# Attention's norms inside the block of delta rule and attention, and the delta queries' norm folded into the out norm

## What is computed

```python
q = l2norm(q) * (Dh ** -0.5)          # l2norm(x) = x * rsqrt(sum(x*x) + 1e-6)
k = l2norm(k)
v_new = u_i - einsum(w_i, S)
o = einsum(q_i * exp(gc_i), S) + einsum(qk_i, v_new)      # qk = q k^T * decay
S = S * gl_i + einsum(kt_i, v_new)
o_a = rms_norm(o_a, out_norm) * silu(z_a)                 # per head; mean over 128 channels, eps 1e-6
```

## Time and profile before

| | |
|---|---|
| median of three runs | 1382.09 us |
| profiled execution | 1383.11 us, span 1381.3 us |
| busy share of the span: TensorE (matmuls / weight loads) | 90% / 74% |
| VectorE / ScalarE / GpSimd | 62% / 35% / 18% |
| norm block | 374.5 to about 402.5 us |
| block of attention and delta rule | about 402.5 to 509.0 us |
| out norm and output projection | from 509.3 us |

### The profile page before, as it was taken

The page is one execution under the profiler, slowest core; times in us unless marked ns, Lnnn a source line. Parts: engine busy times, 40 slices in busy tenths (PEclk is TensorE's granted clock), DMA queues, the critical chain, the costliest instruction groups (busy, mean ns, idle before and its releaser), DMA issues. The chain is left out here.

```text
span 1381.3 us, 20314 instructions
## 1 busy us (share of the span) xinstructions
PE 1238.8 (90%) x8326; PEld 1017.5 (74%) x8326; DVE 856.2 (62%) x1216; ACT 484.0 (35%) x844; POOL 244.3 (18%) x136
## 2 busy tenths in 40 slices
PE   5999999999968989986999999999972579899898
PEld 4677777888647877875888888887651468788787
DVE  5266873761057767226986856595989869555821
ACT  5234236232235674114243221232834422332500
POOL 2222221221003320003221212222320410000000
PEclk9999999999979999998999999999985679999999
DMA  6322121331130022431233252521210000030423
GB/s 203 47 46 57 31 54 46 108 107 32 45 132 1 2 91 78 153 103 36 78 108 104 65 146 55 183 58 58 61 46 0 2 1 1 3 123 1 168 88 111
DMA packets 117556, 97.77 MB, mean 71 GB/s; under 512 B 37016, under 2 KB 102680, under 8 KB 117336
## 3 DMA queue, kind: packets, MB, share of 16 engines
q1 hardware_dynamic: 103832, 77.46, 18.8%
q10 hardware_dynamic: 13632, 19.01, 4.3%
HBM read 70.24 MB, written 24.51 MB: 69 GB/s over the span
## 5 line engine op out<-in xcount | busy, mean ns | idle before, releaser
L178 PE MATMUL banks<-xt_lo,w_hi 128*128 128x512 f32 x816 | 323.8, 397 | 6.0 <-POOL w_lo L529 6.0
L179 PE MATMUL banks<-xt_hi,w_lo 128*128 128x512 f32 x816 | 320.0, 392 | 0.0
L180 PE MATMUL banks<-xt_hi,w_hi 128*128 128x512 f32 x816 | 319.9, 392 | 0.0
L529 POOL TENSOR_TENSOR w_lo<-features,w_hi 128x1024 fp32r<-128x1024 f32 x55 | 147.6, 2685 | 490.3 <-ACT w_hi L539 490.3
L178 PEld LDWEIGHTS banks<-xt_lo,w_hi 128*128 128x128 f32 x816 | 154.7, 190 | 41.5 <-POOL w_lo L529 6.2
L180 PEld LDWEIGHTS banks<-xt_hi,w_hi 128*128 128x128 f32 x816 | 154.5, 189 | 32.6
L179 PEld LDWEIGHTS banks<-xt_hi,w_lo 128*128 128x128 f32 x816 | 154.8, 190 | 31.4
L588 ACT ACTIVATE temporaries<-banks 128x1024 f32<-128x1024 f32 x47 | 56.0, 1192 | 308.1 <-PE banks L180 297.8
L307 PE MATMUL banks<-temporaries,features 128*128 128x128 f32 x256 | 37.9, 312 | 26.2 <-DVE temporaries L284 26.2
L539 ACT ACTIVATE w_hi<-features 128x1024 fp32r<-128x1024 f32 x55 | 57.8, 1054 | 2.0 <-PEq L203 1.0
L178 PE MATMUL banks<-xt_lo,eout_mh 128*128 128x512 f32 x128 | 51.4, 401 | 5.7 <-DVE xt_lo L1727 4.6
(11 more groups left out here) (533 smaller groups left out, 2482.1 us busy)
## 6 DMA issues: line engine op xcount, KB each, us to landing
features<-in_even_w_in SPq DMA_DIRECT2D x26, 512.0 KB, 4.2
features<-in_odd_w_in SPq DMA_DIRECT2D x25, 512.0 KB, 4.9
features<-in_x SPq DMA_DIRECT2D x8, 512.0 KB, 7.7
even_gates<-temporaries ACTq DMA_DIRECT2D x8, 512.0 KB, 2.7
features<-even_gates SPq DMA_DIRECT2D x8, 512.0 KB, 8.7
features<-in_even_w_out SPq DMA_DIRECT2D x8, 512.0 KB, 3.9
temporaries<-in_x SPq DMA_DIRECT2D x8, 512.0 KB, 4.8
h_between_layers<-features SPq DMA_DIRECT2D x8, 512.0 KB, 2.8
```

The source lines that it names most:

```text
L178: nc.tensor.matmul(out, w[0], x[1], start=start, stop=False)
L179: nc.tensor.matmul(out, w[1], x[0], start=False, stop=False)
L180: return nc.tensor.matmul(out, w[0], x[0], start=False, stop=stop)
L529: nc.gpsimd.tensor_tensor(wl[n % 2], wr[n % NW], wh[n % 2].bitcast(F32), ALU.subtract).then_inc(low, 1)
```

## The change

`norm_blocks` goes. Its work on the four attention queries and the key becomes `swa_norms`, a fourth program in the block of attention and delta rule, with due times from -30 to -2; its list of programs is: clearing of semaphores (GpSimd, due -20), `swa_norms`, `swa_attend`, `gdn_state`. The key is scaled first. The banks for the spreads are two pairs, 4 to 7. Every due time of `swa_attend` behind its preparation is raised by 8. The transposes of its values wait for the value's load, all five scalings and `q_kept`. VectorE's copies and SyncE's copies of the key wait for the scaled key, and SyncE issues the bias copies ahead of them. `gdn_state` waits for `gc_by_head` ahead of its first step.

The delta queries are no longer scaled. Their squares (four on ScalarE, due -5) are summed by 16 small matmuls (due -2.5, in bank 6) and kept as `q_squares`, a 128x256 copy by VectorE (due -2). GpSimd's first scaling of the queries waits for the fourth square. In `delta_norm` VectorE adds `q_squares`, times 128 * 128 * 1e-6, to the sums of the output's squares (due 7.5), and the root is taken of this with scale 1/128 and bias 128 * 1e-12.

Cut to its core:

```diff
-def norm_blocks(co, tag, items, params, fetch=(), ahead=(), late=None, expand=None):
+def swa_norms(co, queries, key, gains, loads, later):
...
+    order = [N - 1] + list(range(N - 1))
+    delta_q = co.at(A_F[0], (HG, T))
+    q_sq = [co.at(at, (T,)) for at in (A_T + 2048, A_BIG + 14400)]
+
+    def sync(sp):
+        yield -30
+        sp.dma_start(*loads[0]).then_inc(key_in, 16)
...
+    def scalar(act):
+        yield -30
+        for n, (x, _) in enumerate(items):
+            if n >= 3:
+                act.wait_ge(summed, n - 2)
+            if x is key:
+                act.wait_ge(key_in, 16)
+            nc.scalar.activation(sq[n % 3], x, ACT.Square).then_inc(squared, 1)
+        yield -28
+        act.wait_ge(summed, N)
+        nc.scalar.activation(rows, co.ps[:, 4, 0:Q], ACT.Sqrt, bias=eps, scale=scale).then_inc(rooted, 1)
+        yield -26
+        act.wait_ge(inverted, 1)
+        for q, (_, of) in enumerate(quarters):
+            nc.scalar.activation(high[:, of], rows, ACT.Copy, scale=own_quarter[:, q:q + 1]).then_inc(high_r, 1)
+        yield -5
+        act.wait_ge(low_r, 4)
+        for h in range(HG):
+            if h >= 2:
+                act.wait_ge(q_summed, h - 1)
+            nc.scalar.activation(q_sq[h % 2], delta_q[:, h, :], ACT.Square).then_inc(q_squared, 1)
+
+    def tensor(pe):
+        yield -30
+        for n in range(N):
+            pe.wait_ge(squared, n + 1)
+            for own, of in quarters:
+                last = nc.tensor.matmul(co.ps[own, 4, 0:Q], co.at(A_CST + C_SUM2 + R - 1 - 2 * n, (R,)), sq[n % 3][:, of], start=n == 0, stop=n == N - 1)
+            last.then_inc(summed, 1)
+        for i, n in enumerate(order):
+            yield -5 + 0.2 * i
+            if i == 0:
+                pe.wait_ge(paired, 1)
+                pe.wait_ge(low_r, 4)
+            if i >= 2:
+                pe.wait_ge(normed, i - 1)
+            for h in range(2):
+                out = co.ps[:, 4 + 2 * (i % 2) + h, :]
+                nc.tensor.matmul(out, pairs[:, n, :], low[:, hs[h]], start=True, stop=False)
+                last = nc.tensor.matmul(out, pairs[:, n, :], high[:, hs[h]], start=False, stop=True)
+            last.then_inc(spread, 1)
+        yield -2.5
+        pe.wait_ge(normed, N - 1)
+        for h in range(HG):
+            pe.wait_ge(q_squared, h + 1)
+            for own, of in quarters:
+                last = nc.tensor.matmul(co.ps[own, 6, 0:Q], co.at(A_CST + C_SUM + R - 1 - h, (R,)), q_sq[h % 2][:, of], start=h == 0, stop=h == HG - 1)
+            last.then_inc(q_summed, 1)
+
+    def vector(dve):
+        yield -30
+        by_head_of(co, co.gc_by_head, co.gc_rows).then_inc(expanded, 1)
+        nc.vector.tensor_copy(pairs.rearrange("p i (m c) -> p (i m) c", c=64), bc(co.at(A_CST + C_ROW, (10,)), 64)).then_inc(paired, 1)
+        yield -28
+        dve.wait_ge(rooted, 1)
+        nc.vector.reciprocal(rows, rows).then_inc(inverted, 1)
+        yield -26
+        dve.wait_ge(inverted, 1)
+        for q, (_, of) in enumerate(quarters):
+            dve.wait_ge(high_r, q + 1)
+            nc.vector.scalar_tensor_tensor(low[:, of], rows, own_quarter[:, q:q + 1], high[:, of].bitcast(F32), ALU.mult, ALU.subtract).then_inc(low_r, 1)
+        for i, n in enumerate(order):
+            yield -5 + 0.2 * i
+            x, gain = items[n]
+            dve.wait_ge(spread, i + 1)
+            v = x.rearrange("p (h t) -> p h t", h=2)
+            nc.vector.scalar_tensor_tensor(v, v, gain, co.ps[:, 4 + 2 * (i % 2):6 + 2 * (i % 2), :], ALU.mult, ALU.mult).then_inc(normed, 1)
+        yield -2
+        dve.wait_ge(q_summed, HG)
+        nc.vector.tensor_copy(co.q_squares, co.ps[:, 6, 0:Q]).then_inc(q_kept, 1)
+
+    return dict(sync=sync, scalar=scalar, tensor=tensor, vector=vector, q_squared=(q_squared, HG), q_kept=(q_kept, 1), key_normed=(normed, 1), all_normed=(normed, N), value_in=(value_in, 16), gates_in=(gates_in, 16 * len(loads[2:])),
...
-def gdn_state(co):
+def gdn_state(co, expanded, q_squared):
...
+            if c == 0:
+                pool.wait_ge(*q_squared)
...
+                if c < 0:
+                    pe.wait_ge(*expanded)
...
-def swa_attend(co, sinks, zb, ahead):
+def swa_attend(co, sinks, zb, ahead, norms, late):
...
     def sync(sp):
         yield -9
-            sp.dma_start(kd[64 * h:64 * h + 64, 1 - h, 64:], kb[64 - 64 * h:128 - 64 * h, :]).then_inc(moved, 16)
-        for h in range(2):
+        sp.wait_ge(*norms["key_normed"])
+        for h in range(2):
+            sp.dma_start(kd[64 * h:64 * h + 64, 1 - h, 64:], kb[64 - 64 * h:128 - 64 * h, :]).then_inc(moved, 16)
...
-            yield 10 * n + 2
+            yield late + 10 * n + 2
     def tensor(pe):
-        yield -9
+        yield late - 9
+        pe.wait_ge(*norms["value_in"])
+        pe.wait_ge(*norms["all_normed"])
+        pe.wait_ge(*norms["q_kept"])
-                yield 10 * n + 1
+                yield late + 10 * n + 1
...
-                yield 10 * n + (2 if n >= 0 else 8)
+                yield late + 10 * n + (2 if n >= 0 else 8)
...
-                yield 10 * n + 6
+                yield late + 10 * n + 6
...
     def vector(dve):
-        yield -9
+        yield late - 9
+        dve.wait_ge(*norms["key_normed"])
-        yield -2.5
+        yield late - 2.5
...
-                yield 10 * n + 1
+                yield late + 10 * n + 1
+                if n == 1:
+                    dve.wait_ge(*norms["gates_in"])
-                yield 10 * n + 2
+                yield late + 10 * n + 2
-                yield 10 * n + (3 if n >= 0 else 8)
+                yield late + 10 * n + (3 if n >= 0 else 8)
...
         yield -10
-        yield -7
+        yield late - 7
-                yield 10 * n + (6 if n >= 0 else 8)
+                yield late + 10 * n + (6 if n >= 0 else 8)
-                yield 10 * n + 7
+                yield late + 10 * n + 7
...
-    scale, eps = (co.at(A_CST + C_PARAM + 2 + i, (1,)) for i in range(2))
-    squared, summed, rooted, inverted, high_r, low_r, spread, gated = (
-        co.sem(f"eo_{n}") for n in ("squared", "summed", "rooted", "inverted", "high_r", "low_r", "spread", "gated"))
+    squared, summed, joined, rooted, inverted, high_r, low_r, spread, gated = (
+        co.sem(f"eo_{n}") for n in ("squared", "summed", "joined", "rooted", "inverted", "high_r", "low_r", "spread", "gated"))
     def scalar(act):
...
         yield 8
-        act.wait_ge(summed, N)
-        nc.scalar.activation(rows, co.ps[:, 6, 0:Q], ACT.Sqrt, bias=eps, scale=scale).then_inc(rooted, 1)
+        act.wait_ge(joined, 1)
+        nc.scalar.activation(rows, rows, ACT.Sqrt, bias=co.at(co.eps_at[HEAD * RMS_EPS * L2_EPS], (1,)), scale=1.0 / HEAD).then_inc(rooted, 1)
         yield 11
...
+        yield 7.5
+        dve.wait_ge(summed, N)
+        nc.vector.scalar_tensor_tensor(rows, co.q_squares, HEAD * HEAD * RMS_EPS, co.ps[:, 6, 0:Q], ALU.mult, ALU.add).then_inc(joined, 1)
         yield 9
...
-    co.pairs_r = co.rounded("pairs", A_T + 3072, (5, P))
-    co.eps_at = {RMS_EPS: A_MISC + 568, GN_EPS: A_MISC + 569, 128 * L2_EPS: A_MISC + 570, 64 * RMS_EPS: A_MISC + 571}
+    co.pairs_r = co.rounded("pairs", A_BIG + 13504, (5, P))
+    co.q_squares = co.at(A_T + 3600, (T // 4,))
+    co.eps_at = {RMS_EPS: A_MISC + 568, GN_EPS: A_MISC + 569, 128 * L2_EPS: A_MISC + 570, 64 * RMS_EPS: A_MISC + 571, HEAD * RMS_EPS * L2_EPS: A_MISC + 572}
         def _(pool):
...
-    norm_blocks(co, "eq", [(x_, 64, qn, None) for x_ in qb] + [(kb, 64, kn, None)] + [(x_, 128, 1.0, None) for x_ in q], 0, late=(kb, kvb[0]), expand=(co.gc_by_head, co.gc_rows),
-                fetch=[(vb, kvb[1])] + [(zb[b], zg[WB + b]) for b in range(WB)] + [(za[b], zg[b]) for b in range(WB)])
-    side_by_side(co, swa_attend(co, a["swa_sinks"][0], co.at(A_F[6], (WB, T)), w_ahead), gdn_state(co))
+    cleared = clearing(co, at=-20)
+    norms = swa_norms(co, qb, kb, (qn, kn), [(kb, kvb[0]), (vb, kvb[1])] + [(zb[b], zg[WB + b]) for b in range(WB)], [(za[b], zg[b]) for b in range(WB)])
+    side_by_side(co, cleared, norms, swa_attend(co, a["swa_sinks"][0], co.at(A_F[6], (WB, T)), w_ahead, norms, 8), gdn_state(co, norms["expanded"], norms["q_squared"]))
```

More of the change, by code:

```diff
@@ L654, in _ @@
             aside.upto(NB)
-def norm_blocks(co, tag, items, params, fetch=(), ahead=(), late=None, expand=None):
+def swa_norms(co, queries, key, gains, loads, later):
     nc = co.nc
-    old = co.old_sems() if late is not None else []
     R, Q = 32, T // 4
+    items = [(x, gains[0]) for x in queries] + [(key, gains[1])]
+    N = len(items)
     sq = [co.at(A_T + 1024 * i, (T,)) for i in range(3)]
@@ L668, in norm_blocks @@
     high, low = co.row_parts
-    scale, eps = (co.at(A_CST + C_PARAM + 2 * params + i, (1,)) for i in range(2))
-    first_row = np.cumsum([0] + [P // item[1] for item in items]).tolist()
-    hot, pairs = co.hot_r, co.pairs_r
+    scale, eps = (co.at(A_CST + C_PARAM + i, (1,)) for i in range(2))
+    pairs = co.pairs_r
```

(24 more changed lines are left out.)

8 lines of the change are left out of this document (4 added, 4 removed).

## The result

| | before | after |
|---|---|---|
| median of seven runs | 1382.09 us (1380.71 to 1388.08) | 1390.69 us (1387.81 to 1395.62) |
| ratio after / before, 95% interval | | 1.0057 (1.0038 to 1.0076) |
| profiled execution (span) | 1383.11 (1381.3) | 1393.11 (1391.3) |
| first square of the norms to the end of the last gating | 134.45 | 143.10 |
| the span without that stretch | 1246.9 | 1248.2 |

The change makes the kernel slower by 8.6 us; the forecast was 10 us, 1392. The stretch from the first square (374.56 before, 376.00 after) to the end of the last gating (509.01 before, 519.10 after) is 8.65 us longer, of the 10.0 us between the two spans; the rest of the span differs by 1.3 us. In what follows this stretch is the measure, since single executions reach its first square anywhere between 371.2 and 376.8 us, for reasons that lie before it.

The account below looks back on a forecast made before the run. It took the order of ScalarE's work inside a chunk to bound the kernel as much as TensorE. 412.6 + 16.6 + 70.5 + 19.3 = 519.0 against 509.0, 10 us slower: 1392, range 1380 to 1403.

Parts of the forecast that it names:

- The steady chunk: Mid-block chunk of attention and delta rule: 14.1 us in place of 11.31, so 70.5 from scores 2 to scores 7.
- rival (a): In the block, TensorE stays the bound and the new order costs nothing: faster, 1376; chance 0.12.
- the ring: Chain of waits over TensorE, VectorE and ScalarE from one chunk to the next; 11.31 us before, 14.1 after.
- Attention's norms and the squares: Ahead of the block: four squares leave (3.9 us), delta queries' squares and sums join; first ks at 401.4 instead of 416.97.
- The head: Stretch from first square to the scores of step 1: these at 412.6 instead of 418.5, 5.9 us ahead.
- First pass: First chunks: VectorE's reciprocal of step 0 delays the residual of chunk 1; scores 1 to scores 2 takes 16.6 us.
- rival (c): TensorE's clock falls in the block's new gaps; 16 us more in half of six passes, 1407; chance 0.14.
- Clearing of semaphores: Moves ahead of three memsets on GpSimd; cost between 0 and 20 us, taken as nothing.
- Out norm: One VectorE add ahead of the root, 1.0 us with hand-overs, hidden by 3.2 us of project_out's products.
- (b): Waits in the block partly overlap, ring about 12.3 us, +1 a pass: 1378 to 1386; chance 0.12.
- (d): Norms end last anyway, transposes start at 402.7 not 397.8: 4.9 us more, 1397; within the main case's chance.
- main case: Whole kernel: the ring and first pass as worked out, 1392, range 1387 to 1398; chance 0.62.

Follow-up runs that it names:

- the tie experiment: Changed kernel with one ScalarE due time raised by 0.5, so attention's exponentials come behind the next chunk's decay work: 1386.58 us, 13.57 us a chunk.

## Why the prediction was right

| term | predicted | measured |
|---|---|---|
| first square to scores 1 | 38.0 (374.56 to 412.6) | 35.45 |
| scores 1 to scores 2 | 16.6 | 18.32 |
| scores 2 to scores 7, five chunks | 70.5 (14.1 each) | 70.26 (14.05 each) |
| scores 7 to the end of the last gating | 19.3 | 19.07 |
| sum | 144.4, +10.0 | 143.1, +8.65 |

- *The steady chunk* is the term that decides, and it held in every link of the timeline. That the order is what costs is shown by undoing it (10 in place of 8) and by doing it alone (8 in the kernel before). The case against rival (a) was the ring of the earlier trace rows closing over ScalarE; it stands.
- *Attention's norms and the squares:* parts 3.8 us earlier relative to the first square, copy 0.42 for 0.4. The five scalings took 9.1 us in place of 8.4, so that the third square and the transposes came 0.7 and 0.8 us later than placed. The head was still 2.6 us too dear: I took the transposes at the low clock, 3.55, but TensorE, which had idled 2.63 us ahead of them in the kernel before, idled only 0.64 here and had been busy 3.33 of the 5 us from 395 to 400, the clock was granted in full, and they took 1.94; the first ks and outs, also priced in part at the low clock, gained 1.5 more.
- *First pass:* too cheap by 1.7 us, and one link of it was wrong. The pass does wait for the exponentials of step 0, as I had it, but not through the reciprocal: that is done at 416.88, and the residual starts at 418.14, with TensorE's ks as its releaser. The path goes over ScalarE's copy of the outs, which the new due times put behind those exponentials (6 against 6.5) and for which ks of chunk 1 waits. So from the end of the exponentials to the residual it is 1.7 us, where I had 0.6. TensorE stands idle for 3.4 us, and this once rival (c) came true: the granted clock is 0.80 in the gap and 0.50 in the 4.1 us behind it, where ks takes 2.04 us instead of 1.16. In the two runs with the transposes moved, ks took 1.13 behind the same pause, and from scores 1 to scores 2 it was still 17.97 and 17.91 us; how much of the 1.7 is the clock is not separated. In the steady chunks it stayed at 1.00, as the row with the gap of 1.91 had suggested. What the Trainium skill says in "TensorE: Matmul & The Clock Gate", section What's actually happening, that the low rate is what TensorE falls back to without activity, agrees with the 0.50 behind that gap, though the last section shows that the fall did not come right behind it in every run.
- *Clearing of semaphores:* taken as nothing; GpSimd's first memset came at 382.71, 6.7 us into the block, and nothing waited.
- *Out norm:* the joining took 0.41 us, the parts are ready at 537.68 and TensorE's spreads come at 539.88. The cover was 3.2 us and is 2.2. Counted from the last gating the parts come 0.8 us later, where 1.0 was forecast, and TensorE 0.2 earlier; it cost nothing.
- *Rivals (b) and (d)* did not happen: the waits do not overlap in the changed kernel, and the transposes started 0.8 us late, not the 4.9 of (d). A partial ring near 12 exists with two orders changed back (12.00).
- *Luck:* the forecast of +10.0 is as near to +8.65 as it is because the head, 2.6 us too dear, made up for the first pass, 1.7 too cheap. The chances that I gave add up only roughly: main case and (c) are 0.76, not 0.77.
- What the prediction's reading missed shows in the tie experiment: I listed TensorE's wait for the add as a third small gap and did not ask what stands behind it. In the changed kernel that was free; one edit further it set the time.

*The skill's rule.* "Perfetto Trace Analysis", section Identifying the Most-Contended Engine, in the Trainium skill says which engine to optimise first, the fullest; that a new order would then leave the chunk at 11.3 was my reading of it, as rival (a). The trace disagrees with that reading: the fullest engine stayed TensorE, and 2.74 us a chunk came from the order of the work, with ScalarE busy 7.6 of 14 us. The measurement decides.

## What to carry to other kernels

Where several programs share in-order engines by due times, a constant added to one program changes not only how far it lags but its place among the others' steps modulo the period: write the order of each engine for one period, walk the ring with durations from the trace, and look at ties. A shift by a whole period kept a good order here; a shift by 9 of 10 gave one that was as good, so walk the ring before discarding an order. Look also at the first passes, where a step of the shifted program can come ahead of one that another engine waits for: TensorE's pause of 3.4 us came from one such place on ScalarE. A wait that costs nothing now is worth a line as well, with what is queued behind it: it is what the next edit will run into.

## What was not expected of the hardware

The granted clock did not follow from the length of a pause alone. Gaps of 1.73 and 0.51 us a chunk left it at 1.00 over 70 us. One gap of 2.42 us a chunk stood in five chunks, and around it the clock came down to 0.77 and 0.80 in two of them. The gap of 3.44 us in the first pass brought it to 0.50 right behind it in the changed kernel, and ks took 2.04 us. Behind the same gap in the run without the squares ks ran at full rate:

```profile
412.00 1.13 PE L1221 MATMUL banks<-temporaries,features 128*128 128x128 f32 x8 [3.44 <-ACT features L1323]
```

The runs with the transposes moved had 1.13 there too, and yet their mean from 411 to 425 us is 0.76, as in the changed kernel: the fall came, but later. No run here changes a gap alone, so where and when the clock falls stays open.
